# Residual adds ahead of weight splits at four stage borders of a two-layer encoder trunk

## The reference

```python
for layer in range(DEPTH):                       # DEPTH = 2
    xn = rmsnorm(h, norm_mix_g[layer])
    mix = s5_mlstm_mixer(xn, ...) if layer % 2 == 0 else swa_sink_attention(xn, ...)
    h = h + mix
    h = h + conv_gated_mlp(rmsnorm(h, norm_ffn_g[layer]), ...)
return rmsnorm(h, norm_final_g)

def conv_gated_mlp(xn, w_up, conv_w, conv_b, w_down):
    gate, val = jnp.split(xn @ w_up, 2, axis=-1)  # 2 x 2816 wide
    return (silu(causal_dwconv(gate, conv_w, conv_b)) * val) @ w_down
```

## Time and profile before

| | |
|---|---|
| median of 3 runs | 1130.56 us (1129.69 to 1131.28) |
| the profiled execution | 1132.59 us, of it 1130.8 us span |
| TensorE busy | 1094.9 us, 97% of the span, 5542 matmuls |
| VectorE busy | 649.8 us, 57% |
| ScalarE busy | 465.2 us, 41% |
| GpSimd busy | 208.8 us, 18% |
| mean granted TensorE clock | 0.99 |
| transfers | 106.73 MB, mean 94 GB/s |

### The profile page before, as it was taken

One profiled execution on the slowest core, in us unless ns is written; L12 is line 12 of the kernel. 1 busy time (PEld: TensorE's weight loads), 2 busy tenths in 40 slices (PEclk: granted clock), 3 DMA queues, 4 the chain that ended last, 5 costly groups with the idle time before them and its releaser, 6 DMA issues.

```text
span 1130.8 us, 15508 instructions
## 1 busy us (share of the span) xinstructions
PE 1094.9 (97%) x5542; PEld 883.0 (78%) x5542; DVE 649.8 (57%) x871; ACT 465.2 (41%) x671; POOL 208.8 (18%) x312
## 2 busy tenths in 40 slices
PE   9969998999999999999999999999999999999997
PEld 7847656887888888888887777777888888888886
DVE  6798863556666666653333666266666666652323
ACT  6424553445434443432323365355434444432221
POOL 7998991020000000000000022030000000000000
PEclk9989998999999999999999999999999999999999
DMA  6641200422232222232333211032322223323222
GB/s 218 167 97 60 91 1 1 167 94 94 93 101 103 93 93 93 96 109 98 107 107 116 68 56 57 21 129 94 106 98 93 93 94 103 99 93 112 94 93 75
DMA packets 36491, 106.73 MB, mean 94 GB/s; under 512 B 7840, under 2 KB 10144, under 8 KB 36320
## 3 DMA queue, kind: packets, MB, share of 16 engines
q1 hardware_dynamic: 36448, 106.15, 28.7%
HBM read 101.55 MB, written 3.15 MB: 93 GB/s over the span
## 4 chain that ended last, share of the span: by engine, by line
PE 82%; DVE 4%; ACT 3%; issue 2%; POOL 0%; DVEq 0%; ACTq 0%; POOLq 0%
PE bank L1401 25%; PE bank L1403 25%; PE bank L1402 25%; PE bank L1743 1%; PE bank L1424 1%; ACT whi L645 1%; PE bank L1765 1%; PE bank L1563 1%; DVE h L1217 1%; PE bank L1596 0%; ACT sq L651 0%; PE bank L1543 0%; DVE xlo L949 0%; DVE wlo L943 0%; POOL ssum L435 0%
## 5 line engine op out<-in xcount | busy, mean ns | idle before, releaser
L1401 PE MATMUL bank<-xhi,whi 128*128 128x512 f32 x992 | 391.4, 395 | 7.6 <-DVE xlo L949 2.9
L1402 PE MATMUL bank<-xlo,whi 128*128 128x512 f32 x992 | 386.7, 390 | 0.0
L1403 PE MATMUL bank<-xhi,wlo 128*128 128x512 f32 x992 | 386.6, 390 | 0.0
L943 DVE TENSOR_TENSOR wlo<-raw,whi 128x1024 fp32r<-128x1024 f32 x177 | 223.5, 1263 | 269.0 <-ACT whi L645 268.4
L645 ACT ACTIVATE whi<-raw 128x1024 fp32r<-128x1024 f32 x177 | 187.1, 1058 | 378.3 <-PE bank L1403 350.6
L1401 PEld LDWEIGHTS bank<-xhi,whi 128*128 128x128 f32 x992 | 186.6, 188 | 52.1 <-issue 6.1
L1403 PEld LDWEIGHTS bank<-xhi,wlo 128*128 128x128 f32 x992 | 186.5, 188 | 39.4
L1402 PEld LDWEIGHTS bank<-xlo,whi 128*128 128x128 f32 x992 | 186.6, 188 | 38.6 <-issue 1.0
L1401 PE MATMUL bank<-ahi,whi 128*128 128x512 f32 (+1 forms) x374 | 142.5, 381 | 0.0
L1403 PE MATMUL bank<-ahi,wlo 128*128 128x512 f32 (+1 forms) x374 | 141.6, 379 | 0.0
L1402 PE MATMUL bank<-alo,whi 128*128 128x512 f32 (+1 forms) x374 | 140.4, 375 | 0.0
(11 more groups left out here) (236 smaller groups left out, 1097.4 us busy)
## 6 DMA issues: line engine op xcount, KB each, us to landing
raw<-wstream SPq DMA_DIRECT2D x177, 512.0 KB, 3.3
xin<-xT SPq DMA_DIRECT2D x8, 256.0 KB, 6.1
raw<-wstream SPq DMA_DIRECT2D x8, 256.0 KB, 5.3
h<-xT SPq DMA_DIRECT2D x1, 2048.0 KB, 8.4
outT<-outb SPq DMA_DIRECT2D x8, 256.0 KB, 2.2
u_scratch<-uperm SPq DMA_DIRECT2D x1, 1024.0 KB, 5.6
uc<-u_scratch SPq DMA_DIRECT2D x8, 128.0 KB, 5.2
bcp<-bc SPq DMA_DIRECT2D x1, 512.0 KB, 4.6
```

The source lines that it names most:

```text
L943: V.tensor_tensor(wlo[:, t % RING, :], raw[:, t % RAWS, :], whi[:, t % RING, :].bitcast(f32), ALU.subtract).then_inc(lo_done, 1)
L1401: MM(dst, wh, rhi, start=start, stop=False)
L1402: MM(dst, wh, rlo, start=False, stop=False)
L1403: return MM(dst, wl, rhi, start=False, stop=stop)
```

## The change

`residual_squares` and `residual` are each split into a version for border 1 (`mixed_...`) and one for border 3 (`attended_...`). On VectorE:

- at each block the wait for the tile and the add come first, the weight split after them;
- border 1: `xlo` of blocks 0 to 2 is written before the last add, blocks 3 to 6 behind it;
- border 3: `xlo` of block m follows the add of block m;
- in `down` of both MLPs the add (and in MLP 0 the `xlo`) is ahead of the split of the same step, and so on ScalarE are the square and the `xhi`;
- in attention, `qkv_tile(3)` moves from behind `scores(1)` to ahead of it.

On TensorE the last eight WO blocks of the four open tiles run in another order. On ScalarE the two new functions issue the same instructions in the same order as the one before.

```diff
-        def residual(tiles, splits, o0, g, n):
-
-            for m in range(KB):
-                if m == KB - 1 and n == 1:
-                    dve.wait_ge(out_freed, o0 + KB - 1)
-                    for b in range(KB - 1):
-                        operand_lo(h, g, n, b)
-                wait_tile_used(dve, tiles[m])
-                if m < KB - 1 and splits[m]:
+        def add_residual(tiles, o0, m):
+            wait_tile_used(dve, tiles[m])
+            V.tensor_tensor(h[:, m, :], h[:, m, :], bank[(o0 + m) % 4][:, :], ALU.add).then_inc(out_freed, 1)
+
+        def mixed_residual(tiles, splits, o0, g, n):
+
+            for m in range(KB - 1):
+                add_residual(tiles, o0, m)
+                if splits[m]:
                     split_lo(splits[m])
-                V.tensor_tensor(h[:, m, :], h[:, m, :], bank[(o0 + m) % 4][:, :], ALU.add).then_inc(out_freed, 1)
-                if m and n == 3:
-                    dve.wait_ge(out_freed, o0 + m)
-                    operand_lo(h, g, n, m - 1)
+            dve.wait_ge(out_freed, o0 + KB - 1)
+            for b in range(3):
+                operand_lo(h, g, n, b)
+            add_residual(tiles, o0, KB - 1)
+            for b in range(3, KB - 1):
+                operand_lo(h, g, n, b)
             dve.wait_ge(out_freed, o0 + KB)
             operand_lo(h, g, n, KB - 1)
-            split_lo(splits[-1])
+            split_lo(splits[KB - 1])
+            dve.wait_ge(rstd_done, n + 1)
+
+        def attended_residual(tiles, splits, o0, g, n):
+
+            for m in range(KB):
+                add_residual(tiles, o0, m)
+                if m < KB - 1:
+                    split_lo(splits[m])
+                dve.wait_ge(out_freed, o0 + m + 1)
+                operand_lo(h, g, n, m)
+            split_lo(splits[KB - 1])
             dve.wait_ge(rstd_done, n + 1)
...
             def down(i, last):
                 for s in range(8 if last else 12):
                     wait_tile_used(dve, (d0 + s, i, 12))
-                    if not (last and s >= 8):
-                        split_lo(d0 + s + RING, i, 12)
                     if s % 3 == 2 and not (last and s == 11):
...
+                    if not (last and s >= 8):
+                        split_lo(d0 + s + RING, i, 12)
...
+            if s == 1:
+                qkv_tile(3)
             if s < ITEMS:
                 scores(s)
-            if s % 2 and s < 14:
+            if s % 2 and 1 < s < 14:
                 qkv_tile(3 + s // 2)
...
-        for b in range(6, KB):
-            for m in range(4):
-                ins = wo_block(m, b)
-                if b == KB - 1:
-                    ins.then_inc(tile_used, 1)
+        for m, b in ((0, 6), (1, 6), (0, 7), (1, 7), (2, 6), (2, 7), (3, 6), (3, 7)):
+            ins = wo_block(m, b)
+            if b == KB - 1:
+                ins.then_inc(tile_used, 1)
```

More of the change, by code:

```diff
@@ L835, in _, with fresh_hi, freed_hi, mixed_squares @@
             split_hi(t + RING)
-        def residual_squares(splits, o0, n, g):
+        def fresh_hi(g, m):
+            A(xhi[:, m, :], h[:, m, :], ACT.Copy, scale=col(g, m)).then_inc(xhi_done, 1)
+        def freed_hi(g, b):
+            act.wait_ge(x_free, b + 1)
+            fresh_hi(g, b)
+        def mixed_squares(splits, o0, n, g):
+            for m in range(KB - 1):
+                if splits[m]:
+                    split_hi(splits[m])
+                act.wait_ge(out_freed, o0 + m + 1)
+                square(h[:, m, :], KB * n + m, m % 2)
+            for b in range(KB - 1):
+                freed_hi(g, b)
+            act.wait_ge(out_freed, o0 + KB)
+            fresh_hi(g, KB - 1)
+            square(h[:, KB - 1, :], KB * n + KB - 1, (KB - 1) % 2)
+            split_hi(splits[KB - 1])
+        def attended_squares(splits, o0, n, g):
             for m in range(KB):
-                if m < KB - 1 and splits[m]:
+                if m < KB - 1:
                     split_hi(splits[m])
-                if m == KB - 1 and n == 1:
-                    for b in range(KB - 1):
-                        act.wait_ge(x_free, b + 1)
-                        A(xhi[:, b, :], h[:, b, :], ACT.Copy, scale=col(g, b)).then_inc(xhi_done, 1)
                 act.wait_ge(out_freed, o0 + m + 1)
-                if m == KB - 1 or n == 3:
-                    A(xhi[:, m, :], h[:, m, :], ACT.Copy, scale=col(g, m)).then_inc(xhi_done, 1)
+                fresh_hi(g, m)
                 square(h[:, m, :], KB * n + m, m % 2)
-            split_hi(splits[-1])
+            split_hi(splits[KB - 1])
         def mlp(l):
@@ L866, in down @@
                 for s in range(12):
-                    if not (last and s >= 8):
+                    m = s // 3
+                    ends = s % 3 == 2 and not (last and s == 11)
+                    if not ends and not (last and s >= 8):
                         split_hi(d0 + s + RING, i, 12)
-                    if s % 3 == 2 and not (last and s == 11):
-                        m = s // 3
+                    if ends:
                         act.wait_ge(out_freed, i * 4 + (O_DN[l] + m + 1))
-                        square(h[:, i * 4 + s // 3, :], KB * n + s // 3, (s // 3) % 2, i, 4)
+                        square(h[:, i * 4 + m, :], KB * n + m, m % 2, i, 4)
                         if l == 0:
@@ L883, in mlp @@
                 down(1, True)
-        residual_squares(OUT_SPLITS, O_OUT, 1, "g_ffn0")
+        mixed_squares(OUT_SPLITS, O_OUT, 1, "g_ffn0")
         row_factor(1)
@@ L1293, in _ @@
         dve.wait_ge(x_back, 16)
-        residual(OUT_TILES, OUT_SPLITS, O_OUT, "g_ffn0", 1)
+        mixed_residual(OUT_TILES, OUT_SPLITS, O_OUT, "g_ffn0", 1)
         mlp(0)
```

5 lines of the change are left out of this document (3 added, 2 removed).

## The result

The changed kernel takes 1124.86 us in the median of 5 runs (1123.88 to 1126.64) against 1131.28 us (1129.69 to 1135.12) before: a ratio of 0.9942 with a 95% interval of 0.9927 to 0.9956, 0.44% to 0.73% faster. The forecast was 1122.7 us (1121.2 to 1125.8). The profiled execution took 1125.01 us, 1123.2 us of it span, 7.6 us less than the span before; a step of 7.87 us was forecast. The medians moved by 6.4 us, so the new one lies 2.2 us above the forecast, inside its range.

A forecast was written before the change was run, and what follows sets the result against it. TensorE, busy 97% of the span, was taken as the bound, with 8.57 us of gaps as ceiling. Gains of 1.75 + 1.17 + 0.90 + 1.35 + 2.70 = 7.87 us took the median from 1130.56 to 1122.7 us, range 1121.2 to 1125.8.

The forecast's parts named there:

- Border 1: Norm ahead of MLP 0: add before split gains 1.75 of 2.45 us lost; GpSimd's last add keeps 0.7.
- Border 2: From down of MLP 0 to the first QKV tile: add before split gains the whole 1.17 us.
- Attention: Scores of item 2: QKV tile 3 ahead of the scores of item 1 gains 0.90 us; bounds nothing to 0.90.
- End of the open WO tiles: WO, where the four open tiles end: earlier end of tile 0 and earlier add gain all of 1.35 us.
- Border 3: From the last WO blocks to the mean behind them: add before split lets VectorE catch up, gaining 2.70 us.
- The moved splits: Down of both MLPs: 14 weight splits start 2.0 or 1.3 us later, at cost 0.
- The reserve of the loads: Down stages: the raw slot leaves weight loads 3.8 us to spare, 1.8 after the change.
- the attention chain falling behind: Rival, attention: tile 4 comes late at item 4 and 0.90 us is given back, 1123.6 us; chance 0.12.
- GpSimd in the way: Rival, everywhere: xlo waits for GpSimd's adds eat 5.6 of 7.87 us, 1128.3 to 1130.6 us; chance 0.06.
- Slower by starved splits: Rival, down stages: late loads make moved splits starve TensorE, 1133 us or more; chance 0.04.

The follow-up runs named there:

- the undone run: The changed kernel with QKV tile 3 behind the scores of item 1 again; TensorE's step to item 2 takes 1.22 us against 0.32.
- the run with the longer delay: The changed kernel with four more unused VectorE instructions ahead of each of 14 moved down splits; TensorE's stretches stay at 354.11 and 364.36 us.

## Why the prediction was right

Step by step, what the sum said and what the stretches measured (before less changed):

- Border 1: 1.75 forecast, 9.42 - 7.68 = 1.74 measured. Its two parts are right as well: the earlier start, and 0.7 us kept back by GpSimd's add at xlo 6. The run without that add gains 0.69 more, and so does, with 0.68, the one that has the add and writes the xlo ahead of it. That 0.7 came out so well has some luck in it, as the range given was 0 to 1.4. The gap stands at block 6 only; xlo 7 was in time.
- Border 2: 1.17 forecast, 1.16 measured. xlo 7 ended at 615.41, 1.1 us ahead of TensorE at 616.52; 1.0 was forecast, though the forecast's own times, 616.9 and 618.1, make 1.2.
- Attention: 0.90 forecast and measured. This was the term with the widest bounds (0 to 0.90), and the reason for the upper one, that the chain of items had itself been waiting for TensorE, is what the undone run shows.
- End of the open WO tiles: 1.35 forecast; 112.40 - 111.08 = 1.32 measured. The forecast credited both edits without dividing them; the order of blocks alone is enough, the add alone gives half.
- Border 3: 2.70 forecast, 9.70 - 7.04 = 2.66 measured. The last xlo was done at 754.52, 2.3 us ahead of TensorE at 756.83.
- The moved splits: cost 0 forecast, no difference measured in MLP 1 (364.36 against 364.39 us, spans being rounded to 0.1), and none in MLP 0 beside the gain at its end. The reserve of the loads, put at 1.8 us, was nearer to 2 in MLP 0: 2.4 us more made them late by 0.2 to 0.5.

The five add up to 7.78 us; the part ahead of border 1 took 0.2 us more in the changed kernel's profile, which makes the 7.6 us between the spans. The medians moved by 6.4 us in one comparison and by 7.6 in the other (1131.24 to 1123.64), while the runs of one kernel lie up to 5.4 us apart. So the total confirms the step only roughly, and its nearness to 7.87 proves little; the stretches are the proof. What made the first pair of medians differ by less can't be read, as only one run of each was profiled.

Of the rivals, the attention chain falling behind did not come: tile 4 had more to spare than before. GpSimd in the way was true at border 1, as costed in the forecast, and nowhere else on TensorE's path; the wait is real in other places (the xlo of border 2 took 1.16 us), with time to spare. Slower by starved splits is excluded by the run with the longer delay, up to that delay.

The Trainium skill (SBUF — State Buffer, "Who interferes with whom") says that a VectorE instruction with two SBUF inputs contends with a GpSimd instruction that reads SBUF, over a port that is an exclusive lock. The trace agrees in that one waits for the other: xlo 6 is held up by 1.04 us, four fifths of the 1.3 us that GpSimd's add takes alone.

## What to carry to other kernels

When one engine is busy 97% of the span, the gain of a reordering can be summed from the distances between its starts at the few places where it waits. Here each term held to 0.04 us, because for each place the next thing that is late was worked out too. Put the instruction that frees a buffer or starts the serial chain ahead of the one that only fills a ring with slots to spare. And read a change of a few us in stretches of the trace, between events that both kernels have; the total carries the noise of parts that nobody edited, here above all of a clock that fell in one run and not in the other.

## What the runs showed of the hardware that was not expected

- From border 1 to the end TensorE repeats to 0.03 us per stretch over all twelve profiles, edited places aside, and up to 1110 us its granted clock is 1.00 there in all of them. What differs is the part ahead of it, 246.42 to 251.89 us, in kernels that are alike there except for the order of adds and splits in its last stage. Most of that is the clock in the S5 and mLSTM part. From 150 to 200 us its mean is 0.90 in the profile with 251.89 us, 0.93 in that of the kernel before, 0.97 in both of the changed kernel and 1.00 in the eight others. In those eight TensorE takes 21.23 to 21.27 us from the last pair of matmuls on `emrow` to the first matmul behind the last on `ysb` (175.60 to 196.87 in the run with border 1 undone); it takes 22.58 and 22.87 us at 0.97, 24.18 at 0.93 and 25.71 at 0.90. That is 4.5 of the 5.5 us. Why the clock falls there in some runs is open.
- The pitch of the matmuls depends on the stage: 96 matmuls of WO from 729.63 to 752.03 are 0.233 us each, the 24 behind them 5.48 us to the mean, 0.228 each. The shapes are the same, the operands lie elsewhere. The cause is open.
- GpSimd gets its turn against a stream of VectorE instructions: its add, started amid xlo 5, went ahead of xlo 6 in each of the eight profiles that had this order, and it holds VectorE up for 1.04 us though its own row is 1.3 us long when it runs alone.
- A bias add on VectorE that started at 638.30, while GpSimd was scaling (637.77 to 638.81), took 0.79 us in place of 0.49, and a copy of 128x4 elements 1.05 in place of 0.17. A short instruction can wait almost as long as a large one.
